# Norms and first weight groups in pieces, and one expert pair in four by seven block products

## The reference, cut to what matters

```python
def peer_ffn(hn, w_q, sub_keys, u, v):          # per block of 128 tokens
    q = (xb @ w_q).reshape(p, PEER_HEADS, 2, PEER_QHALF)
    sc = jnp.einsum('thpc,hpnc->thpn', q, sub_keys)
    ...                                          # top 16 of the key pairs, softmax gates
    act = jax.nn.gelu(jnp.einsum('td,ted->te', xb, u[eidx]), approximate=False) * gate
    return jnp.einsum('te,ted->td', act, v[eidx])

def reference(x, ...):
    for l in range(DEPTH):                       # 2 layers
        h = rms_norm(x, norm_mix[l])
        z = h @ w_in[l]
        ...                                      # retention, RWKV-7 and gated linear attention
        x = x + o @ w_out[l]
        h = rms_norm(x, norm_ffn[l])
        x = x + peer_ffn(h, peer_w_q[l], peer_sub_keys[l], peer_u[l], peer_v[l])
    return rms_norm(x, norm_final)
```

## Time and profile before

| | us |
|---|---|
| median of 3 runs | 2188.84 |
| the runs | 2179.97, 2188.84, 2189.22 |
| the profiled execution, its own time | 2180.91 |
| its span, first to last instruction | 2179.1 |
| value product, both layers, two stretches of | about 348 |

### The profile page before, as it was taken

How to read it: one execution, slowest core, us unless ns; L and a number is a source line. 1 busy time by engine, 2 the same in 40 slices (tenths; PEclk the granted TensorE clock), 3 DMA queues, 4 the chain that set the end, 5 groups by cost and what they waited for, 6 DMA issues and landing times.

```text
span 2179.1 us, 45295 instructions
## 1 busy us (share of the span) xinstructions
...
## 2 busy tenths in 40 slices
...
GB/s 210 116 78 1 97 155 165 165 171 157 156 168 157 176 192 192 192 192 192 192 189 97 59 1 98 173 174 166 162 155 170 156 155 191 194 193 192 192 192 184
DMA packets 47464, 338.82 MB, mean 155 GB/s; under 512 B 5649, under 2 KB 5777, under 8 KB 6929
## 3 DMA queue, kind: packets, MB, share of 16 engines
...
...
## 4 chain that ended last, share of the span: by engine, by line
PE 85%; DVE 9%; ACT 2%; DMA 2%; issue 1%; DVEq 0%; SPq 0%; ACTq 0%; PEldq 0%
PE ps L815 11%; PE ps L814 11%; PE ps L816 11%; PE ps L784 10%; PE ps L786 9%; PE ps L785 9%; PE ps L687 3%; PE ps L407 2%; PE ps L408 2%; PE ps L409 2%; PE ps L550 2%; PE ps L564 1%; PE ps L794 1%; PE ps L795 1%; PE ps L423 1%; DVE expert_lo L1320 1%
## 5 line engine op out<-in xcount | busy, mean ns | idle before, releaser
L784 PE MATMUL ps<-h_t_hi,expert_hi 128*128 128x256 f32 x2048 | 591.3, 289 | 12.3 <-DVE expert_lo L1686 8.5
L785 PE MATMUL ps<-h_t_lo,expert_hi 128*128 128x256 f32 x2048 | 578.5, 282 | 0.0
L786 PE MATMUL ps<-h_t_hi,expert_lo 128*128 128x256 f32 x2048 | 578.2, 282 | 0.0
L1869 POOL TENSOR_TENSOR expert_lo<-w_ring,expert_hi 128x512 fp32r<-128x512 f32 x204 | 289.8, 1429 | 772.1 <-ACT expert_hi L975 770.4
L784 PEld LDWEIGHTS ps<-h_t_hi,expert_hi 128*128 128x128 f32 x2048 | 391.6, 191 | 15.6 <-ACT big L980 8.2
L814 PE MATMUL ps<-expert_hi,act_hi 128*128 128x512 f32 x1024 | 398.4, 389 | 0.0
L815 PE MATMUL ps<-expert_lo,act_hi 128*128 128x512 f32 x1024 | 398.4, 389 | 0.0
L816 PE MATMUL ps<-expert_hi,act_lo 128*128 128x512 f32 x1024 | 398.3, 389 | 0.0
L785 PEld LDWEIGHTS ps<-h_t_lo,expert_hi 128*128 128x128 f32 x2048 | 392.0, 191 | 0.0
L786 PEld LDWEIGHTS ps<-h_t_hi,expert_lo 128*128 128x128 f32 x2048 | 391.6, 191 | 0.0
L975 ACT CAST expert_hi<-w_ring 128x512 fp32r<-128x512 f32 x512 | 308.0, 614 | 98.3 <-PE ps L786 83.7
...
## 6 DMA issues: line engine op xcount, KB each, us to landing
w_ring<-u_t SPq DMA_DIRECT2D x128, 1024.0 KB, 4.8
w_ring<-v_t SPq DMA_DIRECT2D x128, 1024.0 KB, 4.8
...
big<-rows SPq DMA_DIRECT2D x2, 576.0 KB, 11.2
```

The costliest lines, as they stand in the source:

```text
L784: pe.matmul(o, w_hi[:, c, :], HTH[:, d, :], start=d == 0, stop=False)
L785: pe.matmul(o, w_hi[:, c, :], HTL[:, d, :], start=False, stop=False)
L786: mm = pe.matmul(o, w_lo[:, c, :], HTH[:, d, :], start=False, stop=d == DC - 1)
L1869: pool.tensor_tensor(EL[:, m % 4, :], RING[:, m // 4, (m % 4) * 512:(m % 4 + 1) * 512], EH[:, m % 4, :].bitcast(F32), ALU.subtract).then_i ...
```

## The change

**The value product.** The first and last body are as before. Between them stand 15 turns k of two bodies each, so four pairs of blocks. The first pair is computed by the scheme of seven block products: with A the activations of two blocks and two tiles and B the two blocks' halves, VectorE makes four sums of activations (s1 to s4, 128 by 128) and four differences of experts (T1 to T4, 128 by 512), each split as before; TensorE makes p1 to p7, three matmuls each, where eight blocks of three stood. p1, p5, p6 and p7 gather in PSUM banks 4 to 7 and are added to x after the loop (`plus`). The other three pairs (c, d, e) have their six matmuls per half. EH and EL get six slots, two of them in `h_t_hi` and `h_t_lo`. Transfers of v come in four pieces of 512 KB.

**Norms and first groups.** Squares go by halves, roots by tiles; TensorE multiplies x by a diagonal with the reciprocal roots, in place of x times them and a plain turn; ScalarE writes h's high part straight from PSUM, VectorE its low part. The first groups of w_in and w_q are split products too. The output product ends tile half by tile half. The keys go to their own place. The pass over w_in's first group stands ahead of the wait for `go`, and its casts and low parts, with the norm, ahead of `arrived`. The last body does tile 0 first. SP clears 40 semaphores in place of 32.

```diff
+V_ORDER = ("p1", "p2", "p3", "c0", "c1", "p7", "c2", "c3", "p6", "d0", "d1", "p5", "d2", "d3", "p4", "e0", "e1", "e2", "e3")
+V_SLOT = (0, 1, 2, 3, 4, 0, 5, 1, 2, 3, 0, 4, 5, 1, 2, 0, 3, 4, 5)
+V_LEN, V_TURNS = len(V_ORDER), N_BODY // 2
+V_ALL = 8 + V_LEN * (V_TURNS - 1) + 8
...
+                    if n == Q_LOAD:
+                        sp.wait_ge(ot_done, 2 * NT)
+                        sp.dma_start(KEYS, keys[l]).then_inc(keys_landed, 16)
...
+                def load_v(c, j):
+                    half = slice(c % 2 * D, (c % 2 + 1) * D)
+                    sp.dma_start(RING[:, c // 2, half], v_t[l, 2 * j + c // 2, :, half]).then_inc(v_landed[c], 16)
...
+                with sp.Fori(1, V_TURNS) as k:
+                    sp.wait_ge(t_made, 4 * k - 1)
+                    load_v(0, 2 * k)
+                    sp.wait_ge(t_made, 4 * k)
+                    load_v(1, 2 * k)
...
+                    sp.wait_ge(v_lo, v_at("e1", k))
+                    load_v(2, 2 * k + 1)
+                    sp.wait_ge(v_lo, v_at("e3", k))
+                    load_v(3, 2 * k + 1)
+                sp.wait_ge(v_lo, V_ALL - 4)
                 first_loads(L - 1)
+                sp.wait_ge(v_lo, V_ALL)
+                second_load(L - 1)
...
-            def turn_h(src, k):
-                for t in range(NT):
-                    pe.wait_ge(h_ready, NT * k + t + 1)
+            def turn_h(k):
+                for t in range(NT):
+                    pe.wait_ge(diag_ready, NT * k + t + 1)
                     for c in range(DC):
-                        mm = pe.transpose(PS[:, 2 * t + c // 4, (c % 4) * P:(c % 4 + 1) * P], src[:, t, c * P:(c + 1) * P], ident)
-                        if c % 4 == 3:
+                        mm = pe.matmul(PS[:, 4 - 4 * k + c // 2, c % 2 * S + t * P:c % 2 * S + (t + 1) * P], X[:, t, c * P:(c + 1) * P], DIAG[:, t, :],
+                                       start=True, stop=True)
+                        if t == NT - 1 and c % 2 == 1:
                             mm.then_inc(h_turned, 1)
...
+                        if k is not None and m < 2:
+                            pe.wait_ge(h_lo, DC * k + d + 1)
                         pe.matmul(o, w_hi_m[:, c, :], HTH[:, d, :], start=d == 0, stop=False)
...
+                for t in range(NT):
+                    for f in range(2):
+                        mm = out_product(5, t, f)
+                mm.then_inc(res_done, 1)
+                out_group_used(2)
+                for t in range(NT):
+                    for f in range(2):
+                        out_product(6, t, f)
+                        out_product(7, t, f).then_inc(res_done, 1)
+                out_group_used(6)
...
+            def v_ending(upto):
+                for t in range(NT):
+                    for m in range(4, 8):
...
+                        if t == NT - 1:
+                            mm.then_inc(v_done, 1)
+                        elif m >= 6:
+                            mm.then_inc(v_top, 1)
...
+            def v_product(name, j, bank, a_hi_t, a_lo_t, start):
+                pe.wait_ge(v_lo, v_at(name, j))
+                o, s = PS[:, bank, :], v_slot(name)
+                pe.matmul(o, a_hi_t, VH[s], start=start, stop=False, skip_group_check=True)
+                pe.matmul(o, a_hi_t, VL[s], start=False, stop=False, skip_group_check=True)
+                pe.matmul(o, a_lo_t, VH[s], start=False, stop=True, skip_group_check=True).then_inc(v_done, 1)
...
+            def v_turn(k, first):
+                pe.wait_ge(a_lo, 8 * k - 3)
+                v_product("p1", k, 4, A11H, A11L, first)
+                pe.wait_ge(a_lo, 8 * k - 2)
+                v_product("p2", k, 0, A2H[:, a12], A2L[:, a12], False)
+                pe.wait_ge(s_lo, k)
+                v_product("p3", k, 1, ASH[:, s4], ASL[:, s4], False)
+                pe.wait_ge(a_lo, 8 * k - 1)
+                v_classic("c0", k, 0, 0)
+                v_classic("c1", k, 0, 1)
+                v_product("p7", k, 7, ASH[:, s3], ASL[:, s3], first)
...
+                v_product("p4", k, 2, A2H[:, a22], A2L[:, a22], False)
+                pe.wait_ge(a_lo, 8 * k + 3)
+                v_classic("e0", k, 0, 0)
+                v_classic("e1", k, 0, 1)
+                pe.wait_ge(a_lo, 8 * k + 4)
+                v_classic("e2", k, 1, 0)
+                v_classic("e3", k, 1, 1)
...
-                turn_h(HN, 0)
-                pe.wait_ge(first_landed, 48 * l + 48)
-                for g in range(3):
+                turn_h(0)
+                group(0)
+                pe.wait_ge(go, l + 1)
+                for g in range(1, 3):
                     group(g)
...
+            def b_high(name, src, j, first):
+                act.wait_ge(v_done, slot_left(name, j, first))
+                act.copy(VH[v_slot(name)], src).then_inc(v_hi, 1)
...
+                left("p1", 1)
+                act.copy(A11H, acts(0, 0, P)).then_inc(a_hi, 1)
+                landed(0, 2 * k - 1)
+                b_high("p1", B11, k, first)
+                landed(1, 2 * k - 1)
+                b_high("p2", B21, k, first)
+                left("p4", 1)
+                act.copy(A2H, acts(1, 0, S)).then_inc(a_hi, 1)
+                act.wait_ge(s_made, 3 * k)
+                left("p5", 1)
+                act.copy(ASH, ASUM).then_inc(s_hi, 1)
+                b_high("p3", B22, k, first)
...
+                act.wait_ge(v_done, v_at("d3", k))
+                act.copy(AH[:, 1, :], acts(7, 0, S)).then_inc(a_hi, 1)
+                b_high("e3", ring(7), k, first)
...
+                for t in range(NT):
+                    for f in range(2):
+                        act.wait_ge(peer_out, 2 * t + f + 1)
+                        squares(0, t, f)
+                    root(0, t)
+                    if t == 0:
+                        act.wait_ge(first_landed, 32 * l + 64)
+                    for m in range(2 * t, 2 * t + 2):
+                        act.wait_ge(v_done, V_ALL - 3 + m)
+                        first_split(m)
+                act.sem_inc(arrived, 1)
...
+            def scaled_diagonal(k, t):
+                a = 8 * k + 2 * t
+                m = 8 * k + 4 + t
+                dve.wait_ge(sumsq_ready, 4 * k + 2 * t + 2)
+                dve.tensor_scalar(STAT[:, m:m + 1], STAT[:, a:a + 1], STAT[:, a + 1:a + 2], NORM_EPS * D, ALU.add, ALU.add).then_inc(rms_ready, 1)
+                dve.wait_ge(rstd_ready, NT * k + t + 1)
+                dve.reciprocal(STAT[:, m + 2:m + 3], STAT[:, m:m + 1]).then_inc(rstd_turned, 1)
+                dve.wait_ge(rstd_turned, NT * k + t + 1)
+                dve.tensor_scalar(DIAG[:, t, :], ident, STAT[:, m + 2:m + 3], None, ALU.mult).then_inc(diag_ready, 1)
...
+            def b_low(name, src, j):
+                dve.wait_ge(v_hi, v_at(name, j))
+                dve.tensor_tensor(VL[v_slot(name)], src, VH[v_slot(name)].bitcast(F32), ALU.subtract).then_inc(v_lo, 1)
...
+                s1, s3, s2, s4 = (ASUM[:, i * P:(i + 1) * P] for i in range(4))
+                dve.tensor_tensor(s3, acts(0, 0, P), acts(0, P, S), ALU.subtract)
+                dve.tensor_tensor(s1, acts(0, P, S), acts(1, P, S), ALU.add).then_inc(s_made, 1)
+                a_low(1, A11L, acts(0, 0, P), A11H)
+                dve.wait_ge(s_made, 3 * k - 2)
+                dve.tensor_tensor(s2, s1, acts(0, 0, P), ALU.subtract).then_inc(s_made, 1)
+                b_low("p1", B11, k)
+                dve.wait_ge(s_made, 3 * k - 1)
+                dve.tensor_tensor(s4, acts(1, 0, P), s2, ALU.subtract).then_inc(s_made, 1)
+                b_low("p2", B21, k)
+                dve.tensor_tensor(T3, B22, B12, ALU.subtract).then_inc(t_made, 1)
+                a_low(2, A2L, acts(1, 0, S), A2H)
+                dve.tensor_tensor(T1, B12, B11, ALU.subtract).then_inc(t_made, 1)
+                dve.wait_ge(s_hi, k)
+                dve.tensor_tensor(ASL, ASUM, ASH.bitcast(F32), ALU.subtract).then_inc(s_lo, 1)
+                dve.wait_ge(t_made, 4 * k - 3)
+                dve.tensor_tensor(T2, T3, B11, ALU.add).then_inc(t_made, 1)
+                b_low("p3", B22, k)
+                dve.wait_ge(t_made, 4 * k - 1)
+                dve.tensor_tensor(T4, B21, T2, ALU.subtract).then_inc(t_made, 1)
+                a_low(3, AL[:, 0, :], acts(2, 0, S), AH[:, 0, :])
...
+                dve.tensor_tensor(T2, T1, PS[:, 7, :], ALU.add).then_inc(folded, 1)
+                dve.wait_ge(folded, 5)
+                plus(x12, PS[:, 5, :])
+                dve.wait_ge(folded, 6)
+                plus(x21, T2)
+                plus(x22, T2)
+                dve.wait_ge(folded, 9)
+                for t in range(NT):
+                    for f in range(2):
+                        if t == 0:
+                            dve.wait_ge(v_top, f + 1)
+                        else:
+                            dve.wait_ge(v_done, V_ALL - 1 + f)
                         xs = X[:, t, f * 512:(f + 1) * 512]
```

(8 more changed lines are left out.)

518 lines of the change are left out of this document (311 added, 207 removed).

## The result

The changed kernel took 2209.0 us (median of 4 runs, 2205.3 to 2212.4), the kernel before 2187.2 us beside it (4 runs, 2180.0 to 2189.2): ratio **1.0107 [1.0084, 1.0129]**, slower by 22 us. The profiled execution had a span of 2210.6 us at a mean granted clock of 0.976; before it was 2179.1 us at 0.986, so the two traces differ by 31.5 us.

The account below looks back on a forecast made before the run. TensorE was taken to bound the kernel, with 85% of the chain. Terms -20.4 + 42 + 1.2 - 3.5 - 14.1 + 0 + 6.0 gave +11.2 us; placed between footings 2192.1 and 2200.0: 2196 us, range 2158 to 2224.

Parts of the forecast that it names:

- the second rival: Value product's turn: short VectorE instructions cost more than their rows, +20 to +40 us beside the forecast, 2215 to 2235; chance 0.17.
- Matmuls and the turn's wait: Value product: 90 matmuls fewer, -20.4 us; TensorE waits at p3 and c0 in thirty turns, +42 us.
- register instructions: VectorE's loop-address instructions before twelve operations of each value-product turn: 0 to 0.03 us each, taken as 0.15 a turn.
- Queries: Norm and first groups before each layer's queries: group 2 starts earlier, -6.2 and -7.9 us.
- Start: Kernel's start, norm and first w_in groups: group 2 starts at 27.8 us instead of 31.0, -3.5 us (-2 to -6).
- Between the layers: Layer boundary: VectorE reports arrival later, group 2 waits for w_in's third part as before; 0 us.
- End: After the last value product: late arrival delays the load of norm_final, +6.0 us.
- the first rival: Value product's turn: TensorE never waits, turn 21.1 to 21.5 us, kernel 2152 to 2172 us; chance 0.25.
- the last rival: Groups 0 and 1 after the boundaries: clock stays at half, at most 6 us there, 3 at the start, 2202; chance 0.08.

Follow-up runs that it names:

- changed_again: The changed kernel, nothing altered, profiled a second time: 2213.1 us, ratio 1.0132 to the kernel before; its profiled execution took 2191.7 us.

## Why the prediction came out as it did

Forecast 2196 us, range 2158 to 2224, slower the likeliest: it came to 2209 us. The forecast difference of spans was +11.2 us. Against it stand +10.1 and +10.7 outside the chunks in the two undisturbed traces, +15.8 at equal clock, +10.8 between the whole traces of before and of changed_again (both near 0.986), and +31.5 with the trace that came first. So the terms are right and the median is not theirs: 2209 lies above the forecast's own 2182 to 2206, and inside the range only because that took in the second rival, costly short instructions, which did not happen (the turn is 22.4 us, not 23 or more). What filled the gap, in the first trace, was chiefly the clock in the chunks (+13.9) and the top-k's loss (5), which the sum did not have. That the range held is luck to this extent; the same kernel's later medians are 2213.1 and 2200.5.

- *Matmuls and the turn's wait.* Right. For the value product of a layer I had -10.2 + 21 + 0.6 = +11.4; without a fall of the clock it is 359.9 - 348.0 = +11.9. The turn is 22.40 us for 22.5. Of the 0.15 us a turn for register instructions some 0.06 were there (22.40 - 21.10 - 1.24). What I missed is the first turn: TensorE waits 1.5 us at p3 there (the 1.5 in the waits above), and in half of the value products the clock then fell for 3 us, 1.4 us more.
- *Queries.* Right to a tenth: forecast -6.2 and -7.9; measured 468.6 - 474.7 = -6.1 and 468.6 - 476.6 = -8.0, where the top-k stage was not disturbed.
- *Start.* Forecast -3.5; -4.3 to -6.5 in the seven later traces of the table. I had the first group begin at 12.5 us and run at half speed until about 20. It begins later, but three matmuls take 0.36 us from the first ones on, which is the full speed of 0.12 each, and group 2 starts at 25.58 instead of 27.8:

```profile
13.98 0.36 PE L464 MATMUL ps<-h_t_hi,expert_hi 128*128 128x256 f32 x1
...
14.42 0.28 PE L464 MATMUL ps<-h_t_hi,expert_hi 128*128 128x256 f32 x1
...
14.78 0.28 PE L464 MATMUL ps<-h_t_hi,expert_hi 128*128 128x256 f32 x1
```

- *Between the layers.* Forecast 0; -1.0 to +0.9. Group 2 starts 25.0 us after the last product, for 25.3 to 26.6 forecast and 25.9 in the earlier trace rows, still behind the load. SyncE's first load comes 2.3 us behind `go` (GpSimd's memset marks it), where I had carried over 2.9 from the kernel before; in all the later traces it is 2.3 to 2.5. What this time consists of, and whether a branch is in it, no run separates:

```profile
1109.05 0.11 POOL L2206 MEMSET big<- 128x4 f32 x1 [373.54 <-SPq L430]
...
1111.33 0.33 SPq L358 DMA_DIRECT2D big<-xconst  x1
...
1125.53 0.39 PE L464 MATMUL ps<-h_t_hi,expert_hi 128*128 128x256 f32 x1 [3.09 <-DVE expert_lo L1513]
```

- *End.* Forecast +6.0, measured +5.1.
- *The step that failed* is the first rival's weight and the last rival's place. I gave TensorE without waits 0.25 because I took the order for given; the forecast on this kernel was right, but the 19.5 us a layer that it costs over 340.4 were a price of order, and three moved operations recover it. And I looked for the clock only behind idle stretches. It fell where TensorE never waited, among the 64-wide matmuls of the chunks, where I had read no row because the change does not touch them. That stretch varies by 9 us a layer from execution to execution of the changed kernel, nearly as much as the whole forecast. The kernel before took anything from 2177.5 to 2198.6 us in 62 executions, so it very likely varies there too; its one trace shows 50.7 and 49.0. The 0.36% between its profiled execution and its median were a sign of it, and I only placed the forecast between the two.
